# Delta-rule levels on half the columns, four 64x64 tiles of the array, and a gate applied in column layout

## The reference, cut to what matters

```python
lhs = eye + einsum("nbhik,nbhjk->nbhij", kb, k) * decay * (1.0 - eye)
u = solve(lhs, v * beta[..., None])          # unit lower triangular
w = solve(lhs, kb * exp(gc)[..., None])
attn = einsum("nbhik,nbhjk->nbhij", q, k) * decay
...
o = (_gated_delta_rule(q, k, v, ...) + _rev(_gated_delta_rule(_rev(q), ...)))
o = _rms(o) * norm_w * silu(z)               # then @ w_out
```

## Time and profile before

| what | value |
|---|---|
| median of 3 runs | 1746.42 us |
| the profiled execution, its own time | 1754.11 us |
| its span in the profile | 1752.3 us |
| mean granted clock of TensorE, share of full | 0.982 |
| RWKV pairs | about 107 to 505 us |
| GDN first head, seven turns, last stage | about 556 to 1287 us |
| one GDN turn (896.94 less 810.25) | 86.7 us |
| its levels, from V of level 1 to the end of T of level 6 (865.40 to 896.94) | 31.5 us |
| output projection, norm, experts | 1287 to 1752 us |

### The profile page before, as it was taken

How to read it: one execution, slowest core, us unless ns; L and a number is a source line. 1 busy time by engine, 2 the same in 40 slices (tenths; PEclk the granted TensorE clock), 3 DMA queues, 4 the chain that set the end, 5 groups by cost and what they waited for, 6 DMA issues and landing times.

```text
span 1752.3 us, 36626 instructions
## 1 busy us (share of the span) xinstructions
PE 1615.6 (92%) x15044; PEld 1017.5 (58%) x15044; DVE 882.4 (50%) x1880; ACT 659.2 (38%) x1316; POOL 122.4 (7%) x311
## 2 busy tenths in 40 slices
PE   6999999999899999999999999999999888777798
PEld 2465565655645667777767676767744544333343
DVE  1372541725423758686868686868610641111163
ACT  2151531515312655555555555555500111111113
POOL 7000010000000000000000000000000022111100
PEclk9999999999999999999999999999999989899999
DMA  9230110301202211111111111111054579999731
GB/s 362 86 99 2 48 49 2 95 0 49 97 19 75 76 50 49 50 49 50 49 50 49 50 49 50 49 50 49 2 204 172 215 292 419 421 421 401 313 154 48
DMA packets 105462, 210.95 MB, mean 120 GB/s; under 512 B 10194, under 2 KB 78135, under 8 KB 92028
## 3 DMA queue, kind: packets, MB, share of 16 engines
q1 hardware_dynamic: 99256, 197.52, 31.1%
q0 software_dynamic: 4896, 8.40, 1.3%
q10 hardware_dynamic: 1188, 3.28, 0.5%
HBM read 203.80 MB, written 14.81 MB: 125 GB/s over the span
## 4 chain that ended last, share of the span: by engine, by line
PE 53%; DMA 10%; DVE 4%; ACT 2%; issue 2%; SPq 0%; DVEq 0%; ACTq 0%; POOL 0%; POOLq 0%
PE ps L1462 12%; DMA W<-in_moe_w_up_dram 7%; PE ps L2501 5%; PE ps L1473 5%; PE ps L1634 4%; PE ps L1603 4%; PE ps L3083 3%; PE ps L2897 3%; DMA W<-in_moe_w_gate_dram 3%; PE ps L506 2%; PE ps L1503 2%; PE ps L1484 1%; PE ps L1513 1%; PE ps L1525 1%; PE ps L1488 1%
## 5 line engine op out<-in xcount | busy, mean ns | idle before, releaser
L1462 PE MATMUL ps<-hT,W 128*128 128x512 f32 x512 | 231.8, 597 | 2.2 <-ACTq L95 2.2
L1462 PEld LDWEIGHTS ps<-hT,W 128*128 128x128 f32 x512 | 95.6, 192 | 99.8 <-issue 98.0
L594 PE MATMUL ps<-hT,W 128*128 128x512 f32 x288 | 138.4, 610 | 4.3 <-DVE spare L189 4.3
L1473 PE MATMUL ps<-W,hT 128*128 128x256 f32 x512 | 126.1, 393 | 0.0
L2045 DVE SCALAR_TENSOR_TENSOR arena<-ps,arena 128x510 f32<-128x510 f32 (+1 forms) x128 | 95.4, 746 | 14.0 <-ACT arena L1764 10.6
L1473 PEld LDWEIGHTS ps<-W,hT 128*128 128x128 f32 x512 | 94.6, 193 | 13.4
L2501 PE MATMUL ps<-W,yT 128*128 128x512 f32 x216 | 93.1, 592 | 0.9 <-ACT yT L1857 0.9
L1867 ACT ACTIVATE W<-ps 128x512 f32<-128x512 f32 x96 | 57.5, 599 | 70.8 <-PE ps L1603 30.7
L594 PEld LDWEIGHTS ps<-hT,W 128*128 128x128 f32 x288 | 50.3, 189 | 51.7 <-issue 49.9
L1634 PE MATMUL ps<-W 64*64 64x64 f32 x2304 | 77.1, 220 | 0.0
L2974 ACT ACTIVATE arena<-arena 128x256 f32<-128x256 f32 x48 | 20.0, 417 | 148.8 <-DVE arena L2611 137.9
(11 more groups left out here) (535 smaller groups left out, 2881.0 us busy)
## 6 DMA issues: line engine op xcount, KB each, us to landing
W<-in_w_in_dram SPq DMA_DIRECT2D x33, 512.0 KB, 6.5
W<-in_gdn_w_in_dram SPq DMA_DIRECT2D x16, 1024.0 KB, 7.5
arena<-in_moe_w_up_dram SPq DMA_DIRECT2D x16, 1024.0 KB, 5.9
arena<-in_moe_w_down_dram SPq DMA_DIRECT2D x16, 1024.0 KB, 9.9
W<-in_moe_w_up_dram SPq DMA_DIRECT2D x16, 1024.0 KB, 5.9
W<-in_moe_w_down_dram SPq DMA_DIRECT2D x16, 1024.0 KB, 5.8
W<-in_moe_w_gate_dram SPq DMA_DIRECT2D x16, 1024.0 KB, 6.0
arena<-in_moe_w_gate_dram SPq DMA_DIRECT2D x14, 1024.0 KB
```

The source lines that it names most:

```text
L594: mm = pe.matmul(ps[:, 5 + i % 2, :], w[:, k, j, :], hT[:, k, :], start=(k == 0), stop=(k == ND - 1))
L1462: mm = pe.matmul(ps[:, 6 + k0 % 2, :], wg[:, k, j * P:(j + 1) * P], hT[:, k, :], start=(k == 0), stop=(k == ND - 1))
L1473: mm = pe.matmul(ps[:, 4 if t < 2 else 1, 256 * (t % 2):256 * (t % 2) + 256], hT[:, k, t * P:(t + 1) * P], wz[:, k, :], start=(k == 0), st ...
```

## The change

It does the following things.

1. Half columns. At level lv only every second block of x columns can change. V takes just these columns of `TTgc` (helper `changing`), 32 rather than 64 per matrix, ScalarE copies half as much, T makes half as much, and `copy_predicated` covers half as much (256 rather than 512 elements for GDN, 128 rather than 256 for RWKV). The mask `quad` is packed to these columns and written out four times. This holds in GDN and in RWKV.
2. Four tiles (GDN only). A group is now reordered: m = 0 to 3 forward, m = 4 to 7 backward (`tile_of`). The products of the backward ones lie off the diagonal of the array (`swapped`), and the order MIXED = 0, 4, 1, 5, ... sets forward and backward side by side, in levels 1 to 4. The forward results go to bank V_BANK[g] (2, 5), the backward ones to the next (3, 6).
3. The transpose of `TTgc` to `Tgc` becomes three, in levels 1 to 3 and in `first_level`: the forward half of all partitions, and the backward half from either half of the partitions to the other. Level 4 keeps one of full width. `first_level` has four masked copies of 128 elements rather than two of 512.
4. Level 6 has no product with the identity and no ScalarE copy; VectorE transposes the one quarter that is missing, behind level 5 (two small transposes for each g in GDN, one for each in RWKV).
5. z is projected as columns: wz stationary, hT streaming 512 columns, half as many products of twice the width, laid in other places of the levels. The weight `gdn_norm_w` enters in `silu_z` as a scalar per partition; `z_weighted` is gone.
6. `gate_ago` only scales. TensorE transposes the scaled output, and VectorE multiplies it by the gate as it takes it from PSUM to `yT` (`gated_y`, two products of 512), behind the first convolution of the turn. ScalarE's `keep_y` is gone. `z_clamped` comes behind it, and `sigmoid_z` behind the first sigmoid.
7. Setup on GpSimd: fewer mask copies. `memset` of TTg in four pieces.

```diff
+def changing(ap, lv, second):
+    return ap.rearrange("p (k s x) -> p k s x", s=2, x=1 << lv)[:, :, second, :]
...
+    V_BANK, T_BANK, TOP_BANK, TOKEN_BANK = (2, 5), (3, 6), (3, 0), (7, 0)
+    def swapped(q, m):
+        return q if m < 4 else HALF[1 - q.start // HD]
+    def half_of(g, m):
+        return ps[:, V_BANK[g] + m // 4, m % 4 * QB:(m % 4 + 1) * QB]
+    MIXED = (0, 4, 1, 5, 2, 6, 3, 7)
...
-                            for m in range(8):
+                            for m in MIXED:
                                 for q in HALF:
-                                    mm = pe.matmul(small(3 * g, m)[q, :], Nn[q, 2 * g + m // 4, m % 4, q], TTgc[q, g, m, :], start=True, stop=True)
+                                    mm = pe.matmul(half_of(g, m)[swapped(q, m), :], Nn[q, g, m, q], changing(TTgc[q, g, m, :], lv, m < 4), start=True, stop=True)
...
-                            mm.then_inc(*s.pe.step(f"Tt {g} {lv}"))
...
+                                for q in HALF:
+                                    of = swapped(q, m)
+                                    mm = pe.matmul(half_of(g, m)[q, :], Tgc[of, g, m, :], Vgh[of, g, m, :], start=True, stop=True)
...
         def put_blocks(s, g, lv):
             hold(dve).then_inc(*s.dve.step())
-            dve.copy_predicated(TTgc[:, g, :, :].rearrange("p (c b) t -> p c b t", c=2), masked(lv), tiles4(ps[:, 3 * g + 2, :]))\
+            dve.copy_predicated(changed(g, lv), quad[:, lv, :, :, :].rearrange("p d n t -> p d (n t)").rearrange("p d (n x) -> p d n x", x=1 << lv),
...
+            if lv < LEVELS - 3:
+                dve.wait_ge(*s.dve.at(f"T {g} {lv}", s.i))
+                for ms, to, of in TURNS:
+                    dve.transpose(Tgc[to, g, ms, :], TTgc[of, g, ms, :]).then_inc(*s.dve.step(f"turned {g} {lv + 1}"))
+            elif lv == LEVELS - 3:
...
+                for d, (of, to), (c0, c1) in ((0, QUARTER[0:2], (QB, 0)), (1, QUARTER[:1:-1], (0, QB))):
+                    dve.transpose(Tgc[to, g, 4 * d:4 * d + 4, c1:c1 + QB], TTgc[of, g, 4 * d:4 * d + 4, c0:c0 + QB]).then_inc(...)
...
+        TURNS = ((slice(0, 4), slice(0, P), slice(0, P)), (slice(4, 8), HALF[1], HALF[0]), (slice(4, 8), HALF[0], HALF[1]))
...
-            dve.tensor_tensor(flat8, flat8, zg.rearrange("p c (e t) -> p (c e) t", e=2), ALU.mult).then_inc(*s.dve.step("ago gated"))
...
+                dve.tensor_tensor(yT[:, k, :], ps[:, 3 + e, :], zg[:, e, :], ALU.mult).then_inc(*s.dve.step(f"{kind}y {e}"))
```

More of the change, by code:

```diff
@@ L320, in _ @@
                 er = slice(e * HD, e * HD + HD)
[L321 to L324, removed]
+                for d, q in ((0, q1), (1, q0)):
+                    own = q[er, er].rearrange("p (k s x) -> p k s x", s=2, x=half)[:, :, 1 - d, :]
+                    link(pool.tensor_copy(quad[er, lv, d, 0, :].rearrange("p (k x) -> p k x", x=half), own))
             pool.wait_ge(*su_pool.last())
+        every = quad.rearrange("p l d n t -> p (l d) n t")
+        link(pool.tensor_copy(every[:, :, 1:4, :], every[:, :, 0:1, :].to_broadcast([P, 2 * (LEVELS - 1), 3, QB])))
+        for d in range(2):
+            link(pool.tensor_copy(first_block[:, d, :, :], quad[:, 0, 1 - d, :, :]))
         su_pool.close()
@@ L1149, in body @@
                     turned(lv + 1)
+                if lv == LEVELS - 2:
+                    for h in range(2):
+                        dve.wait_ge(*rw_dve.at(f"T {h} {lv}", n))
+                        dve.transpose(Tc[QUARTER[1], h, :, 0:QB], TTc[QUARTER[0], h, :, QB:HD]).then_inc(*rw_dve.step(f"turned {h} {lv + 1}"))
                 if lv == 2:
@@ L1306, in build @@
     pcg = take(QUANT, NT, 4)
-    nw = take(P)
+    nw = take(1)
     rsn = take(8)
@@ L1913, in _ @@
             keep_v(s, 0)
+            centre(s, k_)
+            sigmoid(s, k_)
             sigmoid_z(s, 0)
-            centre(s, k_)
-            for e in range(2):
-                keep_y(s, e, True)
-            sigmoid_z(s, 1)
-            sigmoid(s, k_)
             scaled_q(s, 1)
             square(s, k_)
+            sigmoid_z(s, 1)
+            centre(s, q_)
             sigmoid_z(s, 2)
-            centre(s, q_)
             keep_v(s, 1)
@@ L1958, in _ @@
         o_rsqrt(s)
-        for e in range(2):
-            keep_y(s, e, False)
         s.act.close()
@@ L1966, in _ @@
         pool.wait_ge(*ab_pe.at("ab"))
[L1967 to L1969 removed]
+        for g in range(2):
+            for d in range(2):
+                pool.memset(TTg[HALF[1 - d], g, 4 * d:4 * d + 4, HALF[d]], 0.0).then_inc(*ab_pool.step())
                 pool.wait_ge(*ab_pool.last())
@@ L2195, in first_level @@
             for q in HALF:
-                dve.copy_predicated(Tgc[q, g, :, :].rearrange("p (c b) t -> p c b t", c=2), first_block[q, :, :].unsqueeze(1).to_broadcast([HD, 2, 4, HD]),
-                                    Nn[q, 2 * g:2 * g + 2, :, q]).then_inc(*s.dve.step(f"turned {g} 1"))
+                for d in range(2):
+                    ms = slice(4 * d, 4 * d + 4)
+                    to = swapped(q, 4 * d)
+                    dve.copy_predicated(Tgc[to, g, ms, d::2], first_block[to, d, :, :], Nn[q, g, ms, q.start + d:q.stop:2]).then_inc(*s.dve.step(f"turned {g} 1"))
             dve.wait_ge(*s.dve.at(f"turned {g} 1", s.i))
-            dve.transpose(TTgc[:, g, :, :].rearrange("p m t -> p (m t)"), Tgc[:, g, :, :].rearrange("p m t -> p (m t)")).then_inc(*s.dve.step(f"T {g} 0"))
+            for ms, of, to in TURNS:
+                dve.transpose(TTgc[to, g, ms, :], Tgc[of, g, ms, :]).then_inc(*s.dve.step(f"T {g} 0"))
         def levels(s, scan):
@@ L2264, in _ @@
             convolve(s, k_)
+            gated_y(s, True)
+            z_clamped(s)
             output(s, 0)
@@ L2303, in _ @@
         silu_z(s)
-        z_weighted(s)
         output(s, 1)
@@ L2313, in _ @@
         o_normed(s)
-        o_gated(s)
+        gated_y(s, False)
         s.dve.close()
```

210 lines of the change are left out of this document (98 added, 112 removed).

## The result

The changed kernel takes 1777.84 us (median of 4 runs, 1769.03 to 1779.11); the kernel before, beside it, 1749.35. The ratio is 1.0146, 95% interval 1.0125 to 1.0167: slower by 1.5%, where 1725 and a range up to 1750 were predicted. The profiled execution took 1779.11 us, its span is 1777.3, 25.0 more than before. All ratios leave out executions more than 1.5% above the fastest of their kernel: two of the ten of e3 (with them it is 0.9991), one of the ten of e4, and one of the four of e12, which took 2344.2 us at a mean granted clock of 0.642.

A forecast was written before the change was run, and what follows sets the result against it. TensorE, 92% busy, was taken as the bound. Seven heads at 1.9 (13.3), first head 2.5, RWKV 4.2 and last stage 1.2 made 21.2 us off 1754.1: 1732.9, with the median 7.7 lower 1725; range 1706 to 1750.

The forecast's parts named there:

- Four tiles: GDN levels: a group of 32 records takes 0.49 us instead of 0.97, 7.7 us less TensorE work per head.
- Rival B: Tiles sharing row groups don't overlap, so TensorE saves nothing: 0.3 us gained a head, 1738 us; chance 0.10.
- VectorE: GDN levels: three transposes give back more than the narrower copy saves; levels 1 to 3 cost 0.4 us more each.
- the walk: One GDN turn followed in profile times: levels end at 893.0 against 896.94, 3.9 us gained per head before stalls.
- Rival E: VectorE dearer, from short runs or the front losing its cover: +1.5 us a head, 1738 to 1744; chance 0.10.
- the sum of A: The main case, all terms as summed: 1725 us, own range 1714 to 1737; chance 0.55.
- the short runs or a lost cover: Masks with short runs: up to 0.43 us more per copy, taken as nothing; gate's cover gone: some 0.8 a turn.
- Clock: GDN levels: TensorE's waits bring stretches at 1.2 GHz, costing 0.7 us a head, between 0 and 1.7.
- Supply of instructions: GDN levels 2 to 6: late instruction blocks lose 1.3 us per head, bounds 0 and 2.1.
- Rival C: Instruction supply replaces TensorE's work as limit in levels 2 to 6: five stalls of 1.2 us, 1758 us; chance 0.12.
- Gate, z, level 6: Gate's VectorE work hidden by TensorE outside levels; z as columns nothing; GDN level 6's identity product ran beside V.
- sign of error: The prediction is wrong if the turn outside the levels exceeds 55.1 us, or if levels 1 and 2 shrink too.

The follow-up runs named there:

- e3: Changed kernel with one full-width transpose for the three in `first_level` and behind levels 1 to 3, leaving out GDN's backward solution; 0.9969 of the kernel before.
- e4: Changed kernel with only the eight pieces of z moved, into places where TensorE waited; 1.005 of the kernel before.
- e12: The changed kernel run once more, unchanged, beside the others on one chip; 1.0184 of the kernel before.
- e6: Changed kernel with V and T of levels 1 to 4 streaming all 64 columns again, in RWKV and GDN, on four tiles; 1.0038 of the kernel before.
- e5: Kernel before with only the one transpose behind levels 1 to 4 cut into three, on the same partitions; 1.0096 of the kernel before.
- e11: e6 with the edit of e3 (one transpose for three, no GDN backward solution); 0.9829 of the kernel before, 1723.83 us.
- e2: Changed kernel with all tiles of levels 1 to 4 back on the diagonal, one transpose, plain order, half columns kept; 0.9955 of the kernel before.
- e10: e8 with GDN's V and T of levels 1 to 4 streaming 64 columns too, and the MIXED order kept; 0.9868 of the kernel before, 1727.14 us.
- e9: Changed kernel with group g = 0 on the diagonal, g = 1 on four tiles, streaming 64 columns in GDN and RWKV; 0.9878 of the kernel before.
- e1: Kernel before with only the RWKV part of the change (half columns, level 6 without identity products); 0.9996 of the kernel before.
- e7: e1 with RWKV's V and T of levels 1 to 4 streaming all 64 columns; 0.9944 of the kernel before.
- e8: e2 with RWKV streaming 64 columns as in e7, GDN still half columns; 0.9923 of the kernel before.

## Why the prediction was wrong, step by step

**Four tiles: right.** A group was said to take 0.7 us with its latency; it takes 0.67, 15 ns a record. Rival B falls. The rule of the Trainium skill ("TensorE: Matmul & The Clock Gate", "The mechanism") on row groups does not hold in this case: forward and backward tiles share row groups, and a group takes 0.67 us, not 1.15. That columns give TensorE no time on a 64x64 stationary is right too (0.69 us in e6).

**VectorE: the step that failed, by size.** Three transposes were priced at 3 x 0.38; they take 1.42 (so a g has 1.93 for 1.67). The masked copy of level 1, with runs of two elements, takes 0.72 for 0.43: a g has 2.24. The prediction had this doubling as a bound and took nothing, because full-width rows agree; but a full-width copy has no runs. `first_level` takes 3.17 for the 2.5 forecast (2.2 before). Per head: 2 x 0.67 + 2 x 0.57 + 4 x 0.26 = 3.5 us. The profile agrees: in the walk VectorE went from `first_level` to the last copy of level 4 in 23.7 us (862.96 to 886.65); it takes 27.15 (875.81 to 902.96), without a wait. e5 shows the step by itself: three transposes on the same partitions take 1.24, so 0.10 of the 0.28 is in the shapes, and 0.15 comes when two of them go to the other half of the partitions. VectorE had been read as "nearly a second bound" in level 1 and 3, with waits of 1.36 and 1.64 us as its whole room; with that little room each price needed its own row.

**Rival E was the right one, too small.** It added 1.5 a head to the sum of A, clock and supply included, and had a chance of 0.10. 3.5 were needed, and with them the sum gives 1725 + 28 = 1753, outside the range. It took the short runs or a lost cover, not both, and doubted no transpose.

**The sum by place.** In the profiled executions it is off by 46.2 us (21.2 less forecast, 25.0 more measured): 12.8 up to the first head, 33.0 from the first to the last level, 0.4 behind. VectorE's prices make 8 x 3.5 = 28 of the 33.0; the third RWKV pair at half clock makes 12 of the 12.8. The rest is the clock in GDN and what follows from it, less the instructions that TensorE waited for less than forecast; it was not separated further.

**Clock: near in size in GDN, wrong in mechanism, missed in RWKV.** 0.7 us a head was taken; e6 against after gives 8.3 / 8 = 1.0, with 31 us still at half clock. That the size came near is partly luck: the prediction put it down to TensorE's waits, and in e6 the waits are there (58.8 us before V) and most of the half clock is gone. But in RWKV, where nothing makes TensorE wait longer, no clock term stood at all, and the third pair with what follows it took 70.4 us (341.96 to 412.39) for the 58.2 of the second. The reason lay outside the argument: half the columns were "worth nothing". They are worth nothing in TensorE's pace and cost clock. Apart from that RWKV came as forecast: the first two pairs are 1.0 us shorter each, 4.2 were forecast for four.

**Supply of instructions: there, and mostly hidden.** 1.3 us a head was taken, with 2.1 as the bound. In e11 the waits on "issue" are 17.1 us, 2.1 a head: the bound, not the middle. In after they are 3.7 us, 3.1 of them for L1626, less than the 9.4 of before, for TensorE waits for VectorE meanwhile. Rival C falls: its 6.0 a head is not reached even in e11, where TensorE waits least for VectorE of all kernels with four tiles. So the Trainium skill's "mostly hidden" ("Runtime: NRT & Kernel Launch", "Instruction fetch mechanics") holds in after and not in e11.

**Gate, z, level 6: right as far as the traces show.** The stretch between the levels was said to stay 55.1. It is 55.96, which was named as a sign of error; but the 0.8 is `first_level` (3.17 for 2.21), for which V waits. With it back on the diagonal, e2 has 55.0. The last stage gained 0.8 for 1.2.

**The walk itself was not tested with its own prices.** It ended at 27.6 us of levels before stalls, and e3's last head has 27.5. That is partly luck: with one transpose VectorE is cheaper there than the walk had it (1.16 us for a g of level 2 or 3, where the walk had 1.67), and 1.33 us of waits for instructions are in the 27.5. It is luck too that e11 measures 1723.8 where the sum said 1725: e11 gained 28.0 us on its own before (1751.84), and the sum took 21.2 off a median of 1746.42.

A version that beats both kernels came out: e10, 1.3% under before, with half-width copies, no identity product, the gate in columns, tiles on the diagonal, and TensorE streaming the columns it doesn't need. e9 comes to the same within the intervals.

## What to carry to other kernels

When a change moves work from one engine to another whose idle time in the stretch is known (here 3 us of 25), price every new instruction by a row of its own shape, partitions and strides, and let the small costs come true together in the bad case. A reduction that gives the engine no time, such as fewer columns where the pace of the records stays the same, isn't always free: here it paid to leave the columns in and to narrow only the engines that gain. Products on separate tiles should be ordered so that neighbours lie on different ones; levels 5 and 6 gained by that alone, 0.48 and 0.61 us.

## What was not expected of the hardware

- TensorE streaming 32 columns instead of 64, with equal records and pace, the same work of VectorE and waits that were not longer, spent over three times as long at 1.2 GHz (106 us for 31 between the first and the last level). In RWKV it came in some executions only, over 20 us at a time: ten runs of e1 spread over 21 us, four with 64 columns (e7) over 2. 64 columns don't rule such stretches out: in the fourth pair e6 and e9 have 17 us at half clock (0.83 in 51.4 and 51.0 us), and the four runs of e9, e10 and e11 spread over 9, 6 and 14 us.
- `copy_predicated` with runs of two elements took 0.72 us for 256 elements, with runs of four or more 0.42. In RWKV, 128 elements:

```profile
237.26 0.43 DVE L1140 COPY_PREDICATED arena<-quad,ps 128x128 f32<-128x128 uint8 x1
...
240.46 0.28 DVE L1140 COPY_PREDICATED arena<-quad,ps 128x128 f32<-128x128 uint8 x1
```

- A transpose on half the partitions (64x256) took as long as one on all (128x256), 0.44 us. Three in a row took 1.39 us when the two on half the partitions went to the other half of the partitions, and 1.24 in e5 where all stayed. One of 128x512 takes 0.71, less than two of 128x256. The Trainium skill ("VectorE: DVE Perf Modes", section "The TRN2 errata") tells of a fixed cost per instruction that small operands pay again each time; these rows agree.
- In level 6 V took 1.48 us (1.26 in one head of eight) for 1.70, and T 1.15 for 1.54, when successive products alternated between two tiles (e10 for e8).
